# RWKV-7 low-rank products: from mixed inputs to the splits of x and of the token difference

## What is computed

```python
prev = jnp.concatenate([shift_buf[:, None, :], x[:, :-1]], axis=1)
xx = prev - x
xr, xw, xk, xv, xa, xg = [x + xx * mu[i] for i in range(6)]
r = xr @ w_rkv[0]
k = xk @ w_rkv[1]
v = xv @ w_rkv[2]
logw = -jax.nn.softplus(-(w0 + jnp.tanh(xw @ w1) @ w2)) - 0.5
a = jax.nn.sigmoid(a0 + (xa @ a1) @ a2)
g = jax.nn.sigmoid(xg @ g1) @ g2
```

## Time and profile before

| | us |
|---|---|
| median of 3 runs | 3212.39 (3210.69 to 3212.65) |
| profiled execution | 3213.63 |
| its span, first to last instruction | 3211.9 |

### The profile page before, as it was taken

The page is one execution under the profiler, slowest core; times in us unless marked ns, Lnnn a source line. Parts: engine busy times, 40 slices in busy tenths (PEclk is TensorE's granted clock), DMA queues, the critical chain, the costliest instruction groups (busy, mean ns, idle before and its releaser), DMA issues.

```text
span 3211.9 us, 75213 instructions
## 1 busy us (share of the span) xinstructions
PE 2990.8 (93%) x30609; PEld 2820.5 (88%) x30609; DVE 1598.7 (50%) x2375; ACT 1053.5 (33%) x2017; POOL 1310.6 (41%) x911
## 2 busy tenths in 40 slices
PE   6998999976998999989999899989999999899997
PEld 6997999966887887779999699879999899799997
DVE  3336665047036777476640342267661255476612
ACT  3224333234243333243332443343332232433321
POOL 3443444435432223434544244425544334254442
PEclk8998999987998999989999899999999999899998
DMA  7552333522421002322345232243335443133332
GB/s 256 160 189 62 91 93 115 187 67 65 133 72 29 3 3 52 110 62 87 91 126 177 81 123 89 90 158 95 91 104 184 133 132 115 58 93 93 92 91 74
DMA packets 462971, 331.65 MB, mean 103 GB/s; under 512 B 19819, under 2 KB 433465, under 8 KB 462467
## 3 DMA queue, kind: packets, MB, share of 16 engines
q1 hardware_dynamic: 458744, 324.19, 33.0%
q10 hardware_dynamic: 4010, 4.22, 0.5%
HBM read 318.57 MB, written 10.20 MB: 102 GB/s over the span
## 4 chain that ended last, share of the span: by engine, by line
PE 57%; DVE 8%; issue 2%; ACT 2%; DVEq 0%; SPq 0%; DMA 0%; POOL 0%; ACTq 0%
PE bank L1522 31%; PE bank L1530 15%; PE bank L1964 4%; PE bank L1545 1%; DVE h L2428 1%; PE bank L1481 1%; PE bank L1814 1%; DVE mmt L2712 1%; PE bank L1550 1%; DVE proj L2372 0%; PE bank L1610 0%; DVE rw_ST L2733 0%; DVE rstd L2318 0%; DVE mmt L2698 0%; DVE bd_ZR L2669 0%
## 5 line engine op out<-in xcount | busy, mean ns | idle before, releaser
L721 POOL TENSOR_TENSOR w_lo<-w_raw,w_hi 128x1024 fp32r<-128x1024 f32 x406 | 1026.0, 2528 | 1172.4 <-ACT w_hi L899 1172.3
L1522 PE MATMUL bank<-u_hi,w_hi 128*128 128x260 f32 (+2 forms) x4112 | 848.9, 288 | 45.5 <-ACT w_hi L899 22.1
L1522 PE MATMUL bank<-u_lo,w_hi 128*128 128x260 f32 (+2 forms) x4112 | 838.4, 285 | 0.0
L1522 PEld LDWEIGHTS bank<-u_hi,w_hi 128*128 128x128 f32 (+2 forms) x4112 | 635.1, 190 | 64.9 <-issue 44.4
L1522 PEld LDWEIGHTS bank<-u_lo,w_hi 128*128 128x128 f32 (+2 forms) x4112 | 639.2, 189 | 1.8
L899 ACT ACTIVATE w_hi<-w_raw 128x1024 fp32r<-128x1024 f32 x406 | 428.5, 1056 | 478.7 <-PE bank L1530 238.8
L1530 PE MATMUL bank<-u_hi,w_lo 128*128 128x260 f32 (+2 forms) x4112 | 536.0, 283 | 0.0
L1530 PEld LDWEIGHTS bank<-u_hi,w_lo 128*128 128x128 f32 (+2 forms) x4112 | 509.8, 187 | 1.8
L1522 PE MATMUL bank<-hid_hi,w_hi 128*128 128x260 f32 x1664 | 337.6, 284 | 0.0
L1522 PE MATMUL bank<-hid_lo,w_hi 128*128 128x260 f32 x1664 | 335.0, 283 | 0.0
L2862 DVE TENSOR_TENSOR csb<-proj 128x520 f32 (+1 forms) x42 | 30.3, 721 | 486.2 <-ACT proj L964 486.2
(11 more groups left out here) (433 smaller groups left out, 4031.4 us busy)
## 6 DMA issues: line engine op xcount, KB each, us to landing
w_raw<-in_ffn_w_up_dram SPq DMA_DIRECT2D x176, 512.0 KB, 3.7
ada_raw<-in_ada_w_dram SPq DMA_DIRECT2D x132, 512.0 KB, 4.7
w_raw<-in_ffn_w_down_dram SPq DMA_DIRECT2D x64, 448.0 KB, 3.8
w_raw<-in_sconv_w_in_dram SPq DMA_DIRECT2D x48, 512.0 KB, 5.9
w_raw<-in_ffn_w_down_dram SPq DMA_DIRECT2D x32, 512.0 KB, 3.8
ada_pro<-in_ada_w_dram SPq DMA_DIRECT2D x6, 2048.0 KB, 21.3
w_raw<-in_rwkv_w_rkv_dram SPq DMA_DIRECT2D x24, 512.0 KB, 4.8
w_raw<-in_gla_w_in_dram SPq DMA_DIRECT2D x24, 512.0 KB, 4.1
```

Source lines behind the costliest of these rows:

```text
L721: pool.tensor_tensor(w_lo[:, s, :, :], w_raw[:, s, :, :], w_hi[:, s, :, :].bitcast(F32), ALU.subtract).then_inc(lo_done, 1)
L1522: pe.matmul(tile_ps[slot][half][0:width, 0:HALF], w_hi[:, s, k, 0:width], x[:, k0 + k, half * HALF:(half + 1) * HALF], start=start and k = ...
```

## The change

(x + d mu) W is computed as x W + d (mu W), where d is the token difference. For the ranks, W is [w1 | a1] as one block of 128 columns and g1 as a second.

- The pre norm of layer 1 now writes x also as `xb_hi` and `xb_lo`, like the other layers. `gemm_pair(n0)` multiplies x by both blocks as the tiles come, with `stop=False`.
- SP loads the two blocks twice. a1 goes to the right half of slot 0, and SP waits for it (`pack_loaded`) before it loads w1 into the left half. The second copy is multiplied by mu on GpSimd in place (`scale_mix`, three instructions), rounded by ScalarE into `dw_hi` behind the norm's statistics, and its low part `dw_lo` made by GpSimd.
- VectorE writes the difference as eight tiles `rw_d`, ScalarE rounds them into `u_hi`, VectorE subtracts into `u_lo`. A second pair multiplies them by `dw_hi`, `dw_lo` into the same PSUM tiles (`start=False`). TensorE's transposes of `rw_u` stand between the two pairs, and the state row's copy and DMAs on ScalarE behind the second difference tile.
- The mixes w, a and g are gone. r, k and v stay; all their low parts are made on VectorE. Blocks 0 and 1 of r are a pair too, and their weights are rounded while the difference tiles are.
- The ranks are evacuated whole, w and a as one tile of 128 rows. Tanh and sigmoid are applied later, behind the evacuation of block 3 of r.

```diff
-        t_lora = at("t_lora", [HD, 2, T], F32, half_off)
+        t_lora = at("t_lora", [P, T], F32, half_off)
+        dw_hi = at("dw_hi", [P, 2, KT, P], F32R, big_off + 3 * slab_bytes + 8192)
+        dw_lo = at("dw_lo", [P, 2, KT, P], F32R, big_off + 4 * slab_bytes + 2 * T * 4)
...
+            if m < KT:
+                return rw_d[:, m, :]
+            return xf[:, m % 2, :] if m >= 3 * KT or m % 4 < 2 else xf2[:, m % 2, :]
...
-                    for k, src in enumerate((A["rwkv_w1"][j], A["rwkv_a1"][j], A["rwkv_g1"][j][:, 0:HD],
-                                             A["rwkv_g1"][j][:, HD:2 * HD])):
+                    for k in range(4):
...
-                        load_block(n0 + k, k % 2, src.rearrange("(k p) c -> p k c", p=P), HD if k == 3 else 0)
+                        if k % 2:
+                            load_block(n0 + k, 1, A["rwkv_g1"][j].rearrange("(k p) c -> p k c", p=P))
+                        else:
+                            sp.wait_ge(lo_done, n0 + k + 1)
+                            sp.dma_start(w_raw[:, 0, :, HD:P], A["rwkv_a1"][j].rearrange("(k p) c -> p k c", p=P))\
+                              .then_inc(pack_loaded, 16)
+                            sp.wait_ge(pack_loaded, 8 * k + 16)
+                            load_block(n0 + k, 0, A["rwkv_w1"][j].rearrange("(k p) c -> p k c", p=P))
...
-                    mix_low(0)
-                    mix_low(1)
-                    mix_low(2)
-                    low(n0 + 2, 0)
-                    mix_low(3)
-                    low(n0 + 3, 1)
+                    def scale_mix(s, cols, i):
+
+                        c0 = col["rwkv_mu"] + i * KT
+                        w = w_raw[:, s, :, cols]
+                        return pool.tensor_tensor(w, w, vecs[:, c0:c0 + KT].unsqueeze(2).to_broadcast([P, KT, w.shape[2]]),
+                                                  ALU.mult)
+
+                    pool.wait_ge(w_loaded[0], 16 * (n0 // 2 + 1) + 16)
+                    scale_mix(0, slice(0, HD), 1)
+                    scale_mix(0, slice(HD, P), 4).then_inc(scaled, 1)
+                    pool.wait_ge(w_loaded[1], 16 * (n0 // 2 + 1) + 16)
+                    scale_mix(1, slice(0, P), 5).then_inc(scaled, 1)
+                    for s in range(2):
+                        pool.wait_ge(hi_done, n0 + 2 + s + 1)
+                        pool.tensor_tensor(dw_lo[:, s, :, :], w_raw[:, s, :, :], dw_hi[:, s, :, :].bitcast(F32),
+                                           ALU.subtract).then_inc(lo_done, 1)
...
+                        if p["full"]:
+                            act.wait_ge(block_done, n0 + 2)
+                            for s in range(2):
+                                act.wait_ge(scaled, s + 1)
+                                act.activation(dw_hi[:, s, :, :], w_raw[:, s, :, :], ACT.Copy).then_inc(hi_done, 1)
...
+                            act.activation(xb_hi[:, k, 0:TP], normed[:, k % 2, 0:TP], ACT.Identity, **affine)\
+                               .then_inc(uhi_done, 1)
...
+                    mix_high(0, range(0, 2))
+                    rows_to_state()
+                    mix_high(0, range(2, 5))
+                    act.wait_ge(block_done, n0 + 1 + 3)
+                    half_of = lambda _n: n0 // 2 + 2
+                    for s in range(2):
+                        act.wait_ge(w_loaded[s], 16 * (n0 // 2 + 2) + 16)
+                        act.activation(w_hi[:, s, :, :], w_raw[:, s, :, :], ACT.Copy).then_inc(hi_done, 1)
+                    mix_high(0, range(5, KT))
+                    rank_tile(0, t_lora)
+                    rank_tile(1, t_g)
+                    act.sem_inc(lora_copied, 1)
                     mix_high(1)
...
+                            if i == 0 and b == 3:
+                                act.wait_ge(lora_copied, 1)
+                                act.activation(t_lora[0:HD, :], t_lora[0:HD, :], ACT.Tanh)
+                                act.activation(t_g[:, :], t_g[:, :], ACT.Sigmoid)
...
+                    gemm_pair(n0, p["pre"], xb_hi, xb_lo, (u_ready, KT * (p["split"] - 1)), stop=False)
...
+                    gemm_pair(n0 + 2, p["pre"], u_hi, u_lo, (x_ready, 0), (xhi_done, 0), (dw_hi, dw_lo), start=False)
                     pe.wait_ge(urows_copied, 1)
...
-                    for o, i in enumerate((1, 4, 5, 0, 2, 3)):
+                    for o, i in enumerate((None, 0, 2, 3)):
```

165 lines of the change are left out of this document (73 added, 92 removed).

## The result

| | us |
|---|---|
| before | 3212.5 (3210.7 to 3213.2) |
| changed kernel | 3162.3 (3162.1 to 3162.4) |
| ratio | 0.985 (0.983 to 0.986, 95%) |
| forecast | 3180.3, range 3168.0 to 3194.0 |

The direction was right, the size was not. The time lies 18 us under the forecast and 6 us under the range. The profiled execution has a span of 3160.6 us, 51.3 less than before.

The account below looks back on a forecast made before the run. TensorE is 93% busy, so only idle and half-clock time can be won; VectorE and GpSimd pace the low-rank stage. Gains of 30.2 (to r block 3) and 1.9 us (v mixes) sum to 32.1: 3212.4 becomes 3180.3, range 3168.0 to 3194.0.

Parts of the forecast that it names:

- 1. packed loads: Before the low-rank stage: w1 lands near 679.0 behind a1, delaying the squares by 0.2 us, 2.5 if its load is slow.
- 2. scaling on GpSimd: While VectorE makes h: three GpSimd products each hold up one VectorE update, costing 2.6 us, bounds 0 and 4.8.
- 3. low parts against the sample columns: Ahead of the first matmul: GpSimd's two low parts hold up the small sample-column operations, costing 3.1 us, bounds 0 and 4.8.
- 4. pair 1: x with w1, a1, g1: takes 14.4 us, the clock rising inside it, and ends at 722.2.
- 6. pair 2: Difference with scaled weights: VectorE ready at 737.2, TensorE idle about 4 us, then some 3 us at half clock, ending 740.4.
- 7. from there to r block 2: ScalarE's 16 queued mix copies go at VectorE's 1.34 us pace; TensorE goes on at 763.2, the r pair hidden.
- 8. r block 2: Starts at half clock, takes 8.3 us, ends at 771.5: gain 30.2 us; tanh and sigmoid just fit behind block 3.
- 9. v mixes: Behind the end of r: with all subtractions on VectorE the v mixes finish sooner, a gain of 1.9 us.
- A (the lock bites less): Rival for GpSimd's new work: it falls into VectorE's PSUM operations, 8 us more gain, 3172; chance 0.12.
- B: Rival: TensorE stays at half clock through pair 1 and falls behind in pair 2, 9 us less gain, 3190; chance 0.14.
- C: Rival: VectorE bounds the stage as before, only its operation count matters, gain 6 us, 3206; chance 0.03.
- D: Rival, the slower side: the chain of two loads lands w1 late and eats the gain at 33 us late; chance 0.02.

## Why the prediction was wrong, by its own steps

**"TensorE's own work stays"** is the sentence that failed. It counted the 192 matmuls of the first products and never looked at the second ones, those of w2 and a2, though the whole diff has `lora2[rs, ...]` and `t_lora[rs, ...]` with the slot moved from a free dimension to the partitions. It cost the forecast 7.0 us, shown from both sides: taken out of the changed kernel, and put into the kernel before. With this term the forecast would have been some 3173, inside its range. The rest of the miss is of another kind: terms of the sum that were right in the mechanism and too dear by 6.8 us in all (mostly the half clock in steps 4, 6 and 8), and 5.6 us of clock and unexplained time from k block 1 on, for which the sum had nothing. The Trainium skill, "TensorEngine Tiling (Array Packing)", section "Key Properties", says that tiles of the array on different rows work in parallel; the trace agrees, 1.15 us for 2.02. The page names a factor of up to two; here it is 1.76.

| step | forecast | measured |
|---|---|---|
| 1. packed loads | 0.2 | 0.0 |
| 2. scaling on GpSimd | 2.6 | 1.5 |
| 3. low parts against the sample columns | 3.1 | 2.9 |
| first matmul | 707.8 | 706.3 |
| 4. pair 1 | 14.4 | 13.2 |
| 5. transposes | 1.0 | 0.8 |
| 6. pair 2 | 17.2 | 15.0 |
| 7. from there to r block 2 | 22.8 | 22.0 |
| 8. r block 2 | 8.3 | 7.5 |
| 9. v mixes | 1.9 | 1.7 |
| 10. second rank products | not there | 7.0 |

Step 1: w1's high copy ran from 678.89 to 679.95 and the squares started at 680.00, for 679.97 before. The loads came as the step had them, and the cover held by 0.05 us. SP issued w1's load 5.2 us behind a1's, as the row of 5.1 us said, and w1 was there 3.0 us later, at 678.9 for the forecast 679.0:

```profile
670.72 0.43 SPq L557 DMA_DIRECT2D w_raw<-in_rwkv_a_dram  x1
675.89 0.38 SPq L494 DMA_DIRECT2D w_raw<-in_rwkv_w_dram  x1
```

```profile
678.89 1.06 ACT L909 ACTIVATE w_hi<-w_raw 128x1024 fp32r<-128x1024 f32 x1 [7.89 <-DMA w_raw<-in_rwkv_w_dram]
```

The rule of the Trainium skill, "DMA: Bandwidth & Descriptors", section "Anatomy of one DMA", that stands beside this step had both loads in by 676.3; the trace doesn't agree, by 2.6 us. The section gives it for DMAs that GpSimd issues, and these are SP's. That the term came out as 0, as by the rule, is luck.

Step 2: the norm's matmuls moved from 698.63 to 700.12, 1.5 us. Other traces give it a width: from the norm before this one (682.7) it is 15.9 to 16.0 us in the six traces without scalings, and 17.2 to 18.2 in the eight with whole ones, so the scalings cost 1.3 to 2.2. Step 3: from the norm's matmuls to the first matmul of pair 1 it is 6.2 us here and 3.2 in the kernel without GpSimd's work, so 2.9 (2.7 in the changed kernel's second trace). The three scalings gave VectorE three longer updates, and two of them had only 0.13 us more:

```profile
688.25 5.13 POOL L767 TENSOR_TENSOR w_raw<-w_raw,vecs 128x512 f32<-128x512 f32 x3 [3.30 <-DMA w_raw<-in_rwkv_w_dram]
```

```profile
690.76 0.87 DVE L2453 SCALAR_TENSOR_TENSOR h<-proj,mod_f,h 128x512 f32<-128x512 f32 x1
...
692.21 1.72 DVE L2453 SCALAR_TENSOR_TENSOR h<-proj,mod_f,h 128x512 f32<-128x512 f32 x1
...
702.98 2.21 DVE L2419 TENSOR_TENSOR s<-s,mod_m 128x64 f32<-128x64 f32 x1
```

A half-size product mostly fits beside VectorE's 0.7 us in PSUM, so the mechanism was right and the size too large. The last of these rows is step 3: a sample operation of 0.22 us that waited for GpSimd.

Steps 4, 6 and 8: the half clock was priced too dearly each time. Pair 1 was at half clock for 3.6 us only. In pair 2 the gap came as forecast (3.1 us for "about 4"), but the clock stayed at 1.00: the pair ended 1.4 us behind VectorE's last low part (733.8 to 735.2) and not 3.2. The instructions ahead of the gap don't decide this: three of the seven traces that have the same ones ran at half clock there, as I wrote. The ends of my range carried this, but the errors of steps 1 to 8 all had the same sign: 6.8 us in sum.

Step 7 and what hid what: right in the path and the size. The pace was 1.28 us per tile for 1.34, and tanh and sigmoid left no gap. What I called VectorE's pace, though, was priced as a fact of the change, and it was the order of ScalarE's queue that made it bind; that is worth another 11 to 14 us.

Behind step 9 lie 0.9 us at k block 1, at the clock. Windows of TensorE behind that gap, before and changed:

```profile
847.00:853.00 6.00, 6.00 (x28) 0.50 0.30 91
```

```profile
808.00:814.00 6.00, 5.70 (x33) 0.65 0.30 89
```

And the 4.7 us behind the key rows. In the first stretch of it, 2.0 us, the clock is shown. The other 2.7 lie beyond the first scores: 1.1 of them before 1288, where the window of 984 to 1008 shows the clock (0.82 against 0.94), and the rest before 1800. The second traces of both kernels have the same 4.7 in sum. No experiment was made on them, so why the lower level falls otherwise there stays open. No row of before foretells these.

Of the rivals, A (the lock bites less) was nearest, and of its 8 us only 1.3 came (1.1 in step 2, 0.2 in step 3). B, C and D did not happen. That TensorE's own work could change had no rival and no term at all.

## What to carry to other kernels

When an operand's place changes from a free dimension to the partitions, price the matmuls that read it again, even where their number and shape stay; two products that contract over 64 rows ran side by side here when their rows differed. Before a gap is put down to an engine's pace, read what stands in the queue of the engine between: here copies that nobody needed for 40 us held back those that TensorE waited for. And give a gain in the middle of a kernel a margin of some microseconds either way for the clock, which the rows of before don't tell, and compare it at milestones close behind the edit, with two traces of each kernel.

## What the runs showed of the hardware

- A group of four fp32 products that contract over 64 partitions (128 by 260 results, eight records) took 2.02 us with all on partitions 0 to 63, and 1.15 us with two of them on 64 to 127.
- VectorE with two operands in SBUF waits for one GpSimd instruction at a time, and GpSimd for VectorE: eight quarters took 8.80 us where two wholes took 5.19, while VectorE's longest operation fell from 2.83 to 1.2 us. Beside quarters a copy and a cast of 128x64 with one operand in SBUF were held up too: 0.63 and 0.76 us for 0.20 and 0.19.
- Behind the same idle time (3.11 to 3.14 us), with the same instructions ahead of it, the granted clock stayed at 1.0 in four traces and fell to 0.5 in three.
- In four kernels one stretch of 14 to 16 us repeats within 0.1 us from trace to trace; in the two traces of one of them the 2200 us behind it differ by 3.8 us. The Trainium skill, "TensorE: Matmul & The Clock Gate", Part 1, says that the number of slow matmuls at a start varies from run to run of the same kernel. The traces of the changed kernel agree with it: behind the same idle time of 1.5 us, the norm's eight matmuls took 2.10 us in one and 1.16 in the other.
